# A two-block transformer kernel on one core: the first norm's row factors taken out of x and applied to the products

## The chip, the cores and the metric

The kernel runs on one core of a Trainium2 chip. The metric is device time in microseconds (us). One core has TensorE (PE, with its weight loads listed apart as PEld), VectorE (DVE), ScalarE (ACT), GpSimd (POOL), the queue engine SyncE (SP), and 16 DMA engines. SP issues nearly all DMAs. All arithmetic is float32 in meaning; large products are made from "leading" and "trailing" parts in the fp32r format.

## The reference, cut to what matters

Two blocks run one after the other on x, 256 tokens by 1024 features. The change touches the first norm and what is computed from it:

```
h    = x * rsqrt(mean(x*x, -1) + 1e-6) * norm_mix_g        # rmsnorm
proj = h @ w_in            # 1024 x 12296, split into
#  ml_q ml_k ml_v ml_o ml_i ml_f | sc_b sc_c sc_u | sb_q sb_k sb_v | g_ml g_sc g_sb
y_ml = head_rmsnorm(sigmoid(ml_o) * mlstm(ml_q, ml_k, ml_v, ml_i + b_i, ml_f + b_f))
y_sc = sc_b * causal_conv3(sc_c * sc_u)
y_sb = stick_breaking(sb_q, sb_k, sb_v)
merged = sigmoid(g_ml)*(y_ml @ w_ml) + sigmoid(g_sc)*(y_sc @ w_sc) + sigmoid(g_sb)*(y_sb @ w_sb)
x = x + merged @ w_out ; then an MLP, a norm, and a second block of like make-up
```

The factor rsqrt(...) is one number for each token (a "row factor"). As h enters the projections linearly, it can be applied to h or, later, to each product.

## The kernel before, in words

**Units and groups.** Every weight matrix is cut into groups of 512 output columns, and a group into units of up to 4 x 128 input rows. A unit is one 1 MB transfer (4 x 128 x 512 floats) into one of three landing buffers `land`. `UNITS` lists all of them in order, and all engines walk this one list. The first groups are sbq0, sbq1, sbk0, sbk1 and so on, two units each; groups alternate between two halves of the PSUM tensor `acc`.

**What happens to a unit.** SP issues its load (`load(u)`), waiting until the trailing part of unit u-3 is made. ACT copies `land` to `whi` in fp32r (the leading part, `hi_ready`), DVE subtracts it from `land` to get `wlo` (the trailing part, `lo_ready`); both do this in `split(u)`, up to two units ahead of PE. PE then runs `product(u)`. For a "feat" group (output features on partitions) a unit of 4 tiles and 4 column blocks is 48 matmuls of 256 columns: for each tile and block `whi` with `xT_hi`, `whi` with `xT_lo`, `wlo` with `xT_hi`. So all of `whi`, `wlo`, `xT_hi` and `xT_lo` are wanted at once.

**The front.** SP issues x in two halves of 128 tokens (512 KB each), then `con` (identity, triangle and a block of minus ones, 192 KB), then the small vectors (`rows`: 83 rows of 128 floats, 41.5 KB), then units 0 and 1, then five small tensors. ACT sums the squares of x; GpSimd makes `rstd` by `inverse_root`; ACT scales the first 128 tokens of x into `tok` and DVE the other 128. PE transposes the vectors (line 795), DVE copies the result to `vecs`, and PE transposes the scaled x (`turn`, line 591), 16 transposes in four pairs of tiles. `turn_split` turns each pair into `xT_hi` (ACT, times the gain vector) and `xT_lo` (DVE). Unit 0 is split in two halves, so that PE can begin at `half_lo`, the trailing half of the first weight.

```
        pe.wait_ge(norm_act, 1)
        pe.wait_ge(norm_dve, 1)
        pe.wait_ge(vecs_ready, 1)
        turn("x", tok)
```

After unit 0 PE makes a small table from `hot` and `rel33` (line 878); after unit `U_IF` = 1 it makes the two gate rows of the mLSTM (`if_gates`); DVE and ACT work on these at fixed distances from `U_IF`.

**Group ends.** When a group's last unit is done, DVE or ACT reads `acc` in one instruction of 128x1024: a copy or multiplication to sbqT, sbkT, mlqT, mlkT (line 1745), sbv and mlv, cT; an exponential for mlo; a sigmoid for the gates; then the gated products into `tok` (lines 1798 to 1801). The group after the next uses the same half of `acc`. After the last gated product PE transposes `merged` (`turn("merged", tok, half=1)`, inside unit out0) for which it waits on DVE.

**Later norms** already take their factors out of the transposed operand: `make_diag`, `spread` (line 600) and `take_row` turn a column of factors into `row`, the factor of every token on all partitions, which `along` repeats. They run twice, for stages 3 and 5.

The order of the work is written out by hand in the loops over `u`; nothing plans it.

Of the kernel before, what the change touches and what calls it, by code (L numbers as in the profile page):

```python
# [11 lines left out]
P = 128  # L12
# [160 lines left out]
U_IF = 1  # L173
# [9 lines left out]
def build(nc, dram, out):  # L183
# [24 lines left out]
    rstd = sb("rstd", [P, 7, TT], side="right")  # L208
    factor3 = sb("factor3", [P, TT], side="right")
# [141 lines left out]
    norm_act, norm_dve = sem("norm_act"), sem("norm_dve")  # L351
# [112 lines left out]
    def _(pe):  # L464
# [37 lines left out]
        def product(u, between):  # L502
# [12 lines left out]
            if u == 0:  # L515
                pe.wait_ge(half_lo, 1)
            if name == "gu2":
                pe.wait_ge(row_ready, 2)
            for k in range(m):
                if k == (m // 2 if u == 0 else 0):  # L520
# [21 lines left out]
                else:  # L542

                    for c in range(w // P):
# [7 lines left out]
                                  skip_group_check=True)  # L552
            last.then_inc(units_done, 1)
# [226 lines left out]
        def lru_gates():  # L780
            pe.wait_ge(l_conv, 1)
            pe.wait_ge(late_in, LATE)
            pe.wait_ge(row_ready, 1)
# [26 lines left out]
        def between(u, k):  # L810
# [17 lines left out]
            if (u, k) == (B2, 2):  # L828
                pe.wait_ge(xg_ready, 2)
                turn("h3", tok, half=1)  # L830
            if (u, k) == (B2 + 1, 3):
                spread(0, "h3")
# [3 lines left out]
            if (u, k) == (FIRST_U["gu0"] + 1, 2):  # L836
                spread(1, "h4")
# [23 lines left out]
        for u in range(NU):  # L861
# [4 lines left out]
            if u in TILES_APART:  # L866
# [3 lines left out]
                for v in TILES_APART[u]:  # L870
                    tile_product(v, 1).then_inc(units_done, 1)
            else:
                product(u, between)
            if u == 0:
# [33 lines left out]
    def _(act):  # L908
# [33 lines left out]
        def scale(j, src, count):  # L942
            act.wait_ge(rstd_ready, j + 1)
            activate(tok[:, 0, :], src[:, 0, :], ACT.Copy, scale=rstd[:, j, 0:1]).then_inc(norm_act, 1)

        def turn_split(stage, hi, k_to=0, bank=0, half=None):
            _, kk, gain = [s for s in TURNS if s[0] == stage][0]
            more = 2 if stage == "h4" else 0
            for b in range(kk // 2) if half is None else (2 * half, 2 * half + 1):
# [176 lines left out]

        for t in range(TT):
# [17 lines left out]
        for u in range(NU):  # L1145
# [36 lines left out]
            if u == 0:  # L1182
# [3 lines left out]
                             [P, 2 * KD, 8, ML_H]), ACT.Copy).then_inc(if_hi, 1)  # L1186
                act.wait_ge(tab_done, 1)
# [24 lines left out]
            if i == 0:  # L1212
                act.wait_ge(tab_out, 16)
                activate(sums_r[:, :], con[:, K_TRI:K_TRI + 2 * P], ACT.Copy).then_inc(sums_ready, 1)
# [3 lines left out]
            if u - 1 in (LAST_U["mlo0"], LAST_U["mlo1"]):  # L1218
                j = int(u - 1 > LAST_U["mlo0"])
                product_done(f"mlo{j}")  # L1220
                activate(mlo[:, :, j * NG:(j + 1) * NG], acc[:, G_AT[f"mlo{j}"] % 2], ACT.Exp,
                         scale=-1.0).then_inc(read_act, 1)
# [10 lines left out]
            if ends and name[:3] in ("gsb", "gml", "gsc"):  # L1233
# [3 lines left out]
                activate(gate[:], acc[:, n % 2], ACT.Sigmoid).then_inc(read_act, 1)  # L1237
# [66 lines left out]
    def _(dve):  # L1304
# [19 lines left out]
        def scale(j, src):  # L1324
            dve.wait_ge(rstd_ready, j + 1)
            v.tensor_scalar(tok[:, 1, :], src[:, 1, :], rstd[:, j, 1:2], None, ALU.mult).then_inc(norm_dve, 1)

# [763 lines left out]
```

## Time and profile before

| | |
|---|---|
| time, median of 3 runs | 935.81 us (935.42 to 935.91) |
| profiled execution | 935.66 us, span 934.0 us |
| PE busy | 913.2 us, 98% of the span |
| DVE busy | 589.5 us, 63% |
| ACT busy | 478.9 us, 51% |
| DMA | 163.95 MB, mean 176 GB/s |

The span runs from the first to the last recorded instruction; the rest of the time lies around it. PE's busy share is high throughout: in the page's 40 slices only the first (5), the last (7) and one near 735 us (8) are below nine tenths. A timeline row gives start, duration, engine, line, operation, output and inputs, shape and count, and in brackets how long the engine sat idle before and what released it.

### The profile page before, as it was taken

The numbers are of one execution on the slowest core, as the hardware profiler recorded it, in microseconds if no ns is written. First come the engines' busy times: TensorE is split into PE (matmuls) and PEld (weight loads), VectorE is DVE, ScalarE is ACT, GpSimd is POOL, SyncE is SP. The second block draws the span as 40 slices with busy tenths as digits, with TensorE's granted clock in tenths as the row PEclk, the third lists the DMA queues.
The fourth block names the chain that finished last, engine by engine and source line by source line (L and its number), as shares of the span: only waits on it lengthen the run. The fifth ranks groups of instructions, "written<-read, shape, count | busy, mean of one in ns | idle before, by whom it ended". The sixth has DMA issues, their size and how long they took to land.

```text
span 934.0 us, 13028 instructions
## 1 busy us (share of the span) xinstructions
PE 913.2 (98%) x5411; PEld 799.1 (86%) x5411; DVE 589.5 (63%) x619; ACT 478.9 (51%) x539; POOL 44.5 (5%) x88
## 2 busy tenths in 40 slices
PE   5999999999999999999999999999999899999997
PEld 4998998789998888888988888899888798888886
DVE  5555555467887545556677745648886667777643
ACT  6333877883445334334645534356754565555441
POOL 1000111110010000000000000010000100000000
PEclk9999999999999999999999999999999899999999
DMA  8566544544255656555555555537722565555551
GB/s 263 203 229 229 175 137 136 178 136 135 91 181 188 206 193 191 206 189 203 176 184 180 180 189 199 196 96 218 239 91 91 165 197 180 180 181 203 190 170 46
DMA packets 99371, 163.95 MB, mean 176 GB/s; under 512 B 4832, under 2 KB 37315, under 8 KB 99184
## 3 DMA queue, kind: packets, MB, share of 16 engines
q1 hardware_dynamic: 99312, 163.11, 53.1%
q8 instruction: 43, 0.70, 0.3%
q14 instruction: 16, 0.13, 0.0%
HBM read 162.03 MB, written 3.16 MB: 177 GB/s over the span
## 4 chain that ended last, share of the span: by engine, by line
PE 93%; DVE 3%; DMA 1%; ACT 1%; issue 1%; POOL 0%; SPq 0%; DVEq 0%; ACTq 0%; POOLq 0%
PE acc L539 14%; PE acc L541 14%; PE acc L540 14%; PE acc L547 9%; PE acc L551 8%; PE acc L549 8%; PE m L531 7%; PE acc L531 6%; PE m L533 4%; PE acc L533 3%; PE m L591 1%; DMA land<-in_w_in 1%; DVE wlo L1321 1%; PE m L631 1%; PE m L618 1%
## 5 line engine op out<-in xcount | busy, mean ns | idle before, releaser
L1321 DVE TENSOR_TENSOR wlo<-land,whi 128x2048 fp32r<-128x2048 f32 (+2 forms) x153 | 337.4, 2209 | 188.3 <-ACT whi L928 187.8
L928 ACT ACTIVATE whi<-land 128x2048 fp32r<-128x2048 f32 (+2 forms) x153 | 282.0, 1848 | 214.1 <-PE acc L541 152.7
L547 PE MATMUL acc<-xT,whi 128*128 128x256 f32 x656 | 189.9, 289 | 1.3 <-DVE xT L1604 0.8
L551 PE MATMUL acc<-xT,wlo 128*128 128x256 f32 x656 | 186.6, 284 | 0.0
L549 PE MATMUL acc<-xT,whi 128*128 128x256 f32 x656 | 186.6, 284 | 0.0
L547 PEld LDWEIGHTS acc<-xT,whi 128*128 128x128 f32 x656 | 126.7, 193 | 6.5 <-issue 4.4
L549 PEld LDWEIGHTS acc<-xT,whi 128*128 128x128 f32 x656 | 126.8, 193 | 0.2
L551 PEld LDWEIGHTS acc<-xT,wlo 128*128 128x128 f32 x656 | 126.8, 193 | 0.0
L531 PE MATMUL m<-xT,whi 128*128 128x512 f32 x288 | 102.2, 399 | 0.0
L539 PE MATMUL acc<-whi,xT 128*128 128x512 f32 (+2 forms) x240 | 91.5, 381 | 0.0
L540 PE MATMUL acc<-wlo,xT 128*128 128x512 f32 (+2 forms) x240 | 90.2, 376 | 0.0
L541 PE MATMUL acc<-whi,xT 128*128 128x512 f32 (+2 forms) x240 | 90.1, 376 | 0.0
L533 PE MATMUL m<-xT,wlo 128*128 128x256 f32 x288 | 80.9, 281 | 0.0
L531 PE MATMUL acc<-xT,whi 128*128 128x512 f32 x224 | 79.5, 399 | 0.0
L531 PEld LDWEIGHTS m<-xT,whi 128*128 128x128 f32 x288 | 54.1, 188 | 13.4
L533 PE MATMUL acc<-xT,wlo 128*128 128x256 f32 x224 | 62.9, 281 | 0.0
L533 PEld LDWEIGHTS m<-xT,wlo 128*128 128x128 f32 x288 | 54.4, 189 | 0.0
L539 PEld LDWEIGHTS acc<-whi,xT 128*128 128x128 f32 x240 | 45.1, 188 | 9.4 <-issue 1.0
L541 PEld LDWEIGHTS acc<-whi,xT 128*128 128x128 f32 x240 | 45.1, 188 | 8.3
L540 PEld LDWEIGHTS acc<-wlo,xT 128*128 128x128 f32 x240 | 45.1, 188 | 7.8
L531 PEld LDWEIGHTS acc<-xT,whi 128*128 128x128 f32 x224 | 42.1, 188 | 10.5
L539 PE MATMUL acc<-whi,aT_hi 128*128 128x512 f32 x128 | 49.9, 390 | 0.0
(385 smaller groups left out, 1350.8 us busy)
## 6 DMA issues: line engine op xcount, KB each, us to landing
land<-in_w_in SPq DMA_DIRECT2D x56, 1024.0 KB, 5.0
land<-in_w_up SPq DMA_DIRECT2D x16, 1024.0 KB, 5.2
land<-in_w_down SPq DMA_DIRECT2D x16, 1024.0 KB, 5.0
land<-in_w_ffn_gate SPq DMA_DIRECT2D x22, 512.0 KB, 3.7
land<-in_w_ffn_up SPq DMA_DIRECT2D x22, 512.0 KB, 4.7
land<-in_w_ffn_down SPq DMA_DIRECT2D x10, 1024.0 KB, 5.1
land<-in_w_out SPq DMA_DIRECT2D x6, 1024.0 KB, 5.0
land<-in_w_in SPq DMA_DIRECT2D x12, 512.0 KB, 3.7
```

The source lines that it names most:

```text
L531: mm(to, whi[:, s, k, cs], xT[:, k0 + k].rearrange("p a t -> p (a t)"), start=first, stop=False, skip_group_check=True)
L533: last = mm(to[:, 0:T], wlo[:, s, k, cs], xh[:, k0 + k, :], start=False, stop=end, skip_group_check=True)
L539: mm(to, xh[:, k0 + k, ts], whi[:, s, k, 0:w], start=first, stop=False)
L540: mm(to, xh[:, k0 + k, ts], wlo[:, s, k, 0:w], start=False, stop=False)
L541: last = mm(to, xl[:, k0 + k, ts], whi[:, s, k, 0:w], start=False, stop=end)
L547: mm(to, whi[:, s, k, cs], xh[:, k0 + k, :], start=first and c % 2 == 0, stop=False, skip_group_check=True)
L549: mm(to, whi[:, s, k, cs], xl[:, k0 + k, :], start=False, stop=False, skip_group_check=True)
L551: last = mm(to, wlo[:, s, k, cs], xh[:, k0 + k, :], start=False, stop=end, skip_group_check=True)
L591: last = nc.tensor.transpose(M[bank + b][:, (i * TT + t) * P:(i * TT + t + 1) * P], src[:, t, col0 + k * P:col0 + (k + 1) * P], ident)
L618: mm(M[(h + i) % 4][:, 0:T], sbkT[hs, c, 0:P], sbqT[hs, c, :], start=True, stop=True)
L928: activate(whi[:, u % PARTS, 0:m, 0:w], land[:, u % LANDS, 0:m, 0:w], ACT.Copy).then_inc(hi_ready, 1)
L1321: v.tensor_tensor(wlo[:, u % PARTS, 0:m, 0:w], land[:, u % LANDS, 0:m, 0:w], whi[:, u % PARTS, 0:m, 0:w].bitcast(F32), ALU.subtract).then_ ...
```

## The change

- PE transposes x as it came (`turn("x", x_tok)`); both `scale` functions and their semaphores go.
- `con`'s identity and the vectors are issued by ACT ahead of its first activation; `con`'s other two thirds by SP after unit 1.
- Unit 0 comes in two transfers of 512 KB with a semaphore each (`half_in`, `landed[0]`).
- Units 0 and 1 use `first_product`: first all products with the leading part `whi` (pair by pair, `xT_hi` then `xT_lo`), then those with `wlo`. The 48 matmuls of a unit stay 48.
- PE starts with 11 matmuls of 128x512 on a tile of ones, whose results nobody reads.
- The row factors come later: `make_diag(0, 0)`, `spread(0, "x")` after unit 1, `take_row(0)`, its square `row_sq` on DVE, and `minus_rstd` on GpSimd. Feature groups are multiplied by `row` (cT by `row_sq`, which also serves scu; scb's factor goes into psc), token groups are read in two instructions of 128x512 with `rstd` as the scalar.
- `U_IF` goes from 1 to 2, the table product from behind unit 0 to behind unit 1.

```diff
@@ SP
         for t in range(TT):
             sp.dma_start(x_tok[:, t, :], dram["x"][t * P:(t + 1) * P, :]).then_inc(x_in[t], 16)
-        sp.dma_start(con[:], dram["con"]).then_inc(con_in, 16)
-        sp.dma_start(rows[0:V_ROWS, :], dram["vectors"]).then_inc(rows_in, 16)
...
+            if u == 0:
+                (col, w), = segs
+                for half, sem_of in enumerate((half_in, landed[0])):
+                    ks = slice(half * UK // 2, (half + 1) * UK // 2)
+                    sp.dma_start(land[:, 0, ks, :], weights[weight][ks.start * P:ks.stop * P, col:col + w].rearrange(
+                        "(k p) n -> p k n", p=P)).then_inc(sem_of, 16)
+                return
...
             if u == 1:
+                sp.dma_start(con[:, P:], dram["con"][:, P:]).then_inc(ones_in, 16)
@@ PE
+        def first_product(u):
+            s, k0 = u % PARTS, UNITS[u][1]
+            def over(k, weight, moving, opens=False, ends=False):
+                for c in range(NG // P):
+                    to = acc[:, 0, c // 2, (c % 2) * T:(c % 2 + 1) * T]
+                    last = mm(to, weight[:, s, k, c * P:(c + 1) * P], moving[:, k0 + k, :],
+                              start=opens and c % 2 == 0, stop=ends, skip_group_check=True)
+                return last
+            for b in range(UK // 2):
+                if u == 0 and b == 0:
+                    pe.wait_ge(half_hi, 1)
+                else:
+                    pe.wait_ge(hi_ready, u + 1)
+                pe.wait_ge(turn_hi, k0 // 2 + b + 1)
+                for k in (2 * b, 2 * b + 1):
+                    over(k, whi, xT_hi, opens=k0 + k == 0)
+                pe.wait_ge(turn_lo, k0 // 2 + b + 1)
+                for k in (2 * b, 2 * b + 1):
+                    over(k, whi, xT_lo)
+            for k in range(UK):
+                if u == 0 and k == 0:
+                    pe.wait_ge(half_lo, 1)
+                elif k == (UK // 2 if u == 0 else 0):
+                    pe.wait_ge(lo_ready, u + 1)
+                last = over(k, wlo, xT_hi, ends=k0 + k == KD - 1)
+            last.then_inc(units_done, 1)
...
+        pe.wait_ge(heat_set, 1)
+        for _ in range(11):
+            mm(M[3][:, :], ymlT_hi[:, 0, 0:P], ymlT_hi[:, 0:2, :].rearrange("p a b -> p (a b)"), start=True, stop=True)
         pe.wait_ge(con_in, 16)
         pe.wait_ge(rows_in, 16)
         nc.tensor.transpose(M[0][:, 0:V_ROWS], rows[0:V_ROWS, :], ident[0:V_ROWS, 0:V_ROWS]).then_inc(vecs_turned, 1)
-        pe.wait_ge(norm_act, 1)
-        pe.wait_ge(norm_dve, 1)
+        for t in range(TT):
+            pe.wait_ge(x_in[t], 16)
         pe.wait_ge(vecs_ready, 1)
-        turn("x", tok)
+        turn("x", x_tok)
...
+            if (u, k) == (1, UK):
+                pe.wait_ge(ones_in, 16)
+                spread(0, "x")
@@ ACT
+        act.dma_start(con[:, 0:P], dram["con"][:, 0:P]).then_inc(con_in, 16)
+        act.dma_start(rows[0:V_ROWS, :], dram["vectors"]).then_inc(rows_in, 16)
...
-        act.wait_ge(sq_act, 1)
-        scale(0, x_tok, 1)
         act.wait_ge(vecs_ready, 1)
+        turn_split("x", xT_hi, only=(0,))
+        act.wait_ge(half_in, 16)
+        activate(whi[:, 0, 0:UK // 2, :], land[:, 0, 0:UK // 2, :], ACT.Copy).then_inc(half_hi, 1)
+        turn_split("x", xT_hi, only=(1,))
         act.wait_ge(landed[0], land_count(0))
-        activate(whi[:, 0, 0:UK // 2, :], land[:, 0, 0:UK // 2, :], ACT.Copy).then_inc(half_hi, 1)
-        turn_split("x", xT_hi, half=0)
         activate(whi[:, 0, UK // 2:, :], land[:, 0, UK // 2:, :], ACT.Copy).then_inc(hi_ready, 1)
         turn_split("x", xT_hi, half=1)
         split(1)
...
-                activate(gate[:], acc[:, n % 2], ACT.Sigmoid).then_inc(read_act, 1)
+                for t in range(TT):
+                    last = activate(gate[:, t], acc[:, n % 2, t], ACT.Sigmoid, scale=rstd[:, 0, t:t + 1])
+                last.then_inc(read_act, 1)
@@ DVE
-        scale(0, x_tok)
+        dve.wait_ge(vecs_ready, 1)
+        turn_split("x", xT_hi, xT_lo, only=(0,))
         dve.wait_ge(half_hi, 1)
-        dve.wait_ge(landed[0], land_count(0))
+        dve.wait_ge(half_in, 16)
         v.tensor_tensor(wlo[:, 0, 0:UK // 2, :], land[:, 0, 0:UK // 2, :], whi[:, 0, 0:UK // 2, :].bitcast(F32),
                         ALU.subtract).then_inc(half_lo, 1)
-        dve.wait_ge(vecs_ready, 1)
-        turn_split("x", xT_hi, xT_lo, half=0)
+        turn_split("x", xT_hi, xT_lo, only=(1,))
...
         split(1)
+        make_diag(0, 0)
...
+            if u == 1:
+                take_row(0)
+                dve.wait_ge(row_ready, 1)
+                v.tensor_tensor(row_sq[:, :], row[:, :], row[:, :], ALU.mult)
...
-                v.tensor_scalar(to[:, 4 * j:4 * j + 4, :].rearrange("p a b -> p (a b)"), flat, by, None,
-                                ALU.mult).then_inc(read_dve, 1)
+                v.scalar_tensor_tensor(out=to[:, 4 * j:4 * j + 4, :], in0=flat.rearrange("p (a b) -> p a b", b=T),
+                                       scalar=by, in1=along(4), op0=ALU.mult, op1=ALU.mult).then_inc(read_dve, 1)
...
+                    if name[:3] == "psc":
+                        for t in range(TT):
+                            last = v.scalar_tensor_tensor(out=gated[:, t], in0=acc[:, n % 2, t],
+                                                          scalar=rstd[:, 0, t:t + 1], in1=gate[:, t], op0=ALU.mult,
+                                                          op1=ALU.mult)
+                        link(last)
@@ GpSimd
+        signal(g.memset(ymlT_hi[:, 0:2, :].bitcast(F32), 1.0), heat_set)
         link(g.memset(mhalf[:], -0.5))
         signal(g.memset(rel33[BUCKETS:BUCKETS + 1, :], 1.0), pool_set)
         inverse_root(0, [(sq_act, 1)])
+        signal(g.tensor_scalar(minus_rstd[:, :], rstd[:, 0, :], -1.0, None, ALU.mult), minus_ready)
```

## Rows read from the trace of the kernel before

**Rows 1.** The page, part 1: PE's busy time, share and instructions.

```profile
PE 913.2 (98%) x5411; PEld 799.1 (86%) x5411; DVE 589.5 (63%) x619; ACT 478.9 (51%) x539; POOL 44.5 (5%) x88
```

**Rows 2.** Waits: engine, line, what it waited for: us, times, longest.

```profile
PE m L795 <- DMA diag<-in_vectors: 8.8, 1, 8.8
```

**Rows 3.** Timeline of SP, first 12 us.

```profile
0.79 0.86 SPq L398 DMA_DIRECT2D x_tok<-in_x  x2
2.17 0.33 SPq L400 DMA_DIRECT2D diag<-in_vectors  x1
2.54 2.35 SPq L410 DMA_DIRECT2D land<-in_w_in  x2
```

**Rows 4.** Timeline of PE, first 21 us.

```profile
8.81 0.37 PE L795 MATMUL m<-con,diag 83*128 83x83 f32 x1 [8.81 <-DMA diag<-in_vectors]
10.30 3.65 PE L591 MATMUL m<-con,tok 128*128 128x128 f32 x16 [1.12 <-DVE tok L1326]
14.42 0.36 PE L547 MATMUL acc<-xT,whi 128*128 128x256 f32 x1 [0.47 <-DVE xT L1359]
...
20.33 1.02 PE L878 MATMUL m<-hot,rel 33*8 33x512 f32 x2
```

**Rows 5.** Timeline of ACT, first 20 us.

```profile
4.66 1.06 ACT L1129 ACTIVATE tok<-x_tok 128x1024 f32<-128x1024 f32 x1 [2.60 <-DMA x_tok<-in_x]
...
6.00 1.06 ACT L1129 ACTIVATE tok<-x_tok 128x1024 f32<-128x1024 f32 x1 [0.18 <-DMA x_tok<-in_x]
...
11.17 1.06 ACT L1139 ACTIVATE whi<-land 128x1024 fp32r<-128x1024 f32 x1 [1.58 <-DMA land<-in_w_in]
12.14 1.55 ACT L957 ACTIVATE xT<-m,vecs 128x256 fp32r<-128x256 f32 x4
...
15.93 3.77 ACT L928 ACTIVATE whi<-land 128x2048 fp32r<-128x2048 f32 x2
```

**Rows 6.** DMA view, packets by size: 6.5 to 8.0 us, then 8.0 to 8.5.

```profile
DMA packets 299, 0.53 MB, mean 353 GB/s; under 512 B 0, under 2 KB 54, under 8 KB 299
DMA packets 89, 0.18 MB, mean 356 GB/s; under 512 B 2, under 2 KB 2, under 8 KB 89
```

**Rows 7.** Timeline of DVE, 9 to 23 us.

```profile
9.30 0.24 DVE L1639 COPY vecs<-m 128x83 f32<-128x83 f32 x1 [3.02 <-PE m L795]
9.46 0.74 DVE L1326 TENSOR_SCALAR tok<-x_tok,rstd 128x1024 f32<-128x1024 f32 x1
...
13.41 1.65 DVE L1359 SCALAR_TENSOR_TENSOR xT<-m,vecs,xT 128x256 fp32r<-128x256 f32 x4
...
17.92 4.49 DVE L1321 TENSOR_TENSOR wlo<-land,whi 128x2048 fp32r<-128x2048 f32 x2 [0.16 <-ACT whi L928]
```

**Rows 8.** Transposes of line 591 (ns min/median/max): of x at 10.3, of mlo at 277 us.

```profile
L591 PE MATMUL m<-con,tok x16: 421/421/447, 10.3 to 13.5; 128*128 128x128 f32 x16
L591 PE MATMUL m<-con,mlo x16: 272/272/273, 277.6 to 279.2; 128*128 128x128 f32 x16
```

**Rows 9.** Timeline of GpSimd at 8 us.

```profile
8.41 0.52 POOL L1968 MEMSET sel_r<- 36x512 f32 x1
```

**Rows 10.** Windows on PE: stretch, length, busy (count), granted clock, DMA share, GB/s.

```profile
734.40:739.56 5.16, 1.97 (x10) 0.85 0.57 197
739.56:744.60 5.04, 5.04 (x23) 0.50 0.00 0
```

**Rows 11.** Timeline of PE around the first spread.

```profile
630.75 0.61 PE L600 MATMUL m<-diag,con 128*128 128x128 f32 x4
631.12 0.36 PE L547 MATMUL acc<-xT,whi 128*128 128x256 f32 x1
```

**Rows 12.** Groups on DVE by form: count, busy us, mean ns, idle before.

```profile
L1620 DVE SCALAR_TENSOR_TENSOR mixed<-acc,rstd,gain_b 128x512 f32<-128x512 f32 x4 | 2.9, 748 | 9.5 <-ACT tok L985 9.5
```

**Rows 13.** Timeline of DVE and PE behind the last gated product.

```profile
418.03 1.22 DVE L1801 TENSOR_TENSOR tok<-tok,gated 128x1024 f32<-128x1024 f32 x1
...
419.31 1.09 PE L591 MATMUL m<-con,tok 128*128 128x128 f32 x8
```

More of the change, by code:

```diff
@@ L172 @@
 GATE0 = SB0 + SB_H
-U_IF = 1
+U_IF = 2
 TURN_SB = ML0 + 6
@@ L208, in build @@
     rstd = sb("rstd", [P, 7, TT], side="right")
+    minus_rstd = sb("minus_rstd", [P, TT], side="right")
+    row_sq = sb("row_sq", [P, T], side="right")
     factor3 = sb("factor3", [P, TT], side="right")
@@ L830, in between @@
                 turn("h3", tok, half=1)
+            if (u, k) == (1, UK):
+                pe.wait_ge(ones_in, 16)
+                spread(0, "x")
             if (u, k) == (B2 + 1, 3):
-                spread(0, "h3")
+                spread(1, "h3")
             if (u, k) == (FIRST_U["gu0"], 2):
@@ L836, in between @@
             if (u, k) == (FIRST_U["gu0"] + 1, 2):
-                spread(1, "h4")
+                spread(2, "h4")
             if (u, k) == (B2 + 4, 4):
@@ L940, in square, with turn_split @@
             act.wait_ge(sq_act, squares_done[0])
[L942 to L946, printed above, removed]
+        def turn_split(stage, hi, k_to=0, bank=0, half=None, only=None):
             _, kk, gain = [s for s in TURNS if s[0] == stage][0]
             more = 2 if stage == "h4" else 0
-            for b in range(kk // 2) if half is None else (2 * half, 2 * half + 1):
+            for b in only or (range(kk // 2) if half is None else (2 * half, 2 * half + 1)):
                 act.wait_ge(turned, TURN_AT[stage] + b + 1 + more)
@@ L1220, in _ @@
                 product_done(f"mlo{j}")
-                activate(mlo[:, :, j * NG:(j + 1) * NG], acc[:, G_AT[f"mlo{j}"] % 2], ACT.Exp,
-                         scale=-1.0).then_inc(read_act, 1)
+                act.wait_ge(minus_ready, 1)
+                for t in range(TT):
+                    last = activate(mlo[:, t, j * NG:(j + 1) * NG], acc[:, G_AT[f"mlo{j}"] % 2, t], ACT.Exp,
+                                    scale=minus_rstd[:, t:t + 1])
+                last.then_inc(read_act, 1)
             if i % 2 == 1 and 3 <= i <= SB_H + 1:
@@ L1345, in along, with turn_split @@
             return row[:, :].unsqueeze(1).to_broadcast([P, k, T])
-        def turn_split(stage, hi, lo, k_to=0, bank=0, half=None):
+        def turn_split(stage, hi, lo, k_to=0, bank=0, half=None, only=None):
             _, kk, gain = [s for s in TURNS if s[0] == stage][0]
             more = 2 if stage == "h4" else 0
-            for b in range(kk // 2) if half is None else (2 * half, 2 * half + 1):
+            for b in only or (range(kk // 2) if half is None else (2 * half, 2 * half + 1)):
                 dve.wait_ge(turn_hi, TURN_AT[stage] + b + 1 + more)
@@ L1666, in _ @@
                 turn_split("h3", xT_hi, xT_lo, half=1)
-                make_diag(0, 3)
+                make_diag(1, 3)
             if u == FIRST_U["gu0"]:
@@ L1672, in _ @@
                 turn_split("h4", xT_hi, xT_lo, half=1)
-                make_diag(1, 5)
+                make_diag(2, 5)
             if u - SB0 in range(4, SB_H + 3, 2):
@@ L1749, in _ @@
                 product_done(name)
-                if name[0] == "s":
-                    last = v.tensor_copy(sbv[:, :, j * NG:(j + 1) * NG], acc[:, n % 2])
-                else:
+                if name[0] == "m":
                     v.memset(mlv[:, :, 2 * j:2 * j + 2, ML_D:ML_D + 1], 1.0)
-                    last = v.tensor_copy(mlv[:, :, 2 * j:2 * j + 2, 0:ML_D],
-                                         acc[:, n % 2].rearrange("p t (h d) -> p t h d", d=ML_D))
+                for t in range(TT):
+                    if name[0] == "s":
+                        to, src = sbv[:, t, j * NG:(j + 1) * NG], acc[:, n % 2, t]
+                    else:
+                        to = mlv[:, t, 2 * j:2 * j + 2, 0:ML_D]
+                        src = acc[:, n % 2, t].rearrange("p (h d) -> p h d", d=ML_D)
+                    last = v.tensor_scalar(to, src, rstd[:, 0, t:t + 1], None, ALU.mult)
                 last.then_inc(read_dve, 1)
@@ L1799, in _ @@
                 else:
-                    link(v.tensor_tensor(gated[:], acc[:, n % 2], gate[:], ALU.mult))
+                    if name[:3] == "psc":
+                        for t in range(TT):
+                            last = v.scalar_tensor_tensor(out=gated[:, t], in0=acc[:, n % 2, t],
+                                                          scalar=rstd[:, 0, t:t + 1], in1=gate[:, t], op0=ALU.mult,
+                                                          op1=ALU.mult)
+                        link(last)
+                    else:
+                        link(v.tensor_tensor(gated[:], acc[:, n % 2], gate[:], ALU.mult))
                     v.tensor_tensor(m, m, gated[:], ALU.add).then_inc(read_dve, 1)
```

36 lines of the change are left out of this document (19 added, 17 removed).

## Prediction

> **What bounds the kernel now.** The page first: PE is busy 98% of the span [rows 1], so only PE's stalls and added or removed PE work can move the time. The waits view comes next: its longest entry on PE is 8.8 us before the first transpose, for the DMA of the vectors [rows 2]. The rest is in the timeline of the first 20 us, engine by engine. The SP timeline [rows 3] gives the issue order x, x, (con,) vectors, first weight. The vectors' transpose starts at 8.81, the 16 transposes of x at 10.30, the first product at 14.42, and from there PE runs without a gap until the table product at 20.33 [rows 4]. So the front of 14.42 us is the prize; everything in the change outside it can only cost.
>
> Why do the vectors land at 8.78 although they were issued at 2.17, when the second half of x, issued under a microsecond earlier, is used at 6.00 [rows 3, 5]? The DMA view: from 6.5 to 8.0 us 54 packets of 512 B pass, and none of that size from 8.0 to 8.5 [rows 6]. That is 28 ns each, 18 GB/s: about what one of 16 engines moves when all move 353 GB/s (22 each), not what 16 would. So I take it that the 83 rows of the vectors run on one engine, 83 x 28 ns = 2.3 us, done at 8.0, landing 0.8 later. It also explains why ACT gets the 1 MB weight only at 11.17, 8.6 us after its issue [rows 3, 5]: on that engine it starts at 8.0 and takes 64 KB at some 25 GB/s, 2.6 us. The Trainium skill (DMA: Bandwidth & Descriptors, section "Why a DMA increments its semaphore by 16 and not by 1") says the number of engines is the largest up to 16 that divides the outer dimension, so that 83, a prime, gets one; by that rule too moving the issue to another queue spreads nothing.
>
> **The change part by part.** Start of the chain. Norm: the row factors leave the front: DVE's scaling of 9.46 to 10.20 was what the transposes waited for [rows 7], and ACT's, as long, goes too. The transposes now need x, con and the vectors. The con part before them is a third (64 of 192 KB; 128 KB at 0.4 MB per us is 0.3 us). Issuing from ACT saves no engine work: the one engine still has to move its part of x, con and all 83 rows before the transposes can start. So the later of x and vectors lands at 8.78 - 0.3 = 8.5. Low bound: the 83 rows cost nothing, which leaves x and con, 6.2; high bound under the rivals.
>
> From there: before, landing to the end of the vecs copy was 9.54 - 8.78 = 0.76 [rows 7], plus 0.08 to wake PE: transposes start at 9.35 (before 10.30, after DVE's scaling). Four transposes take 0.6 us at the full clock (16 records in 1.91 at 277 us is 0.107 apart plus the tail; 272 ns each [rows 8]), 1.1 at half (421 ns [rows 8]). ACT then splits the first pair, half of 1.55, 0.78, and copies half a weight, 1.06 [rows 5]; with 0.15 for semaphores the leading half is ready at 9.35 + 0.6 + 0.78 + 1.06 + 0.15 = 11.95. (Where x is the later of the two, ACT has its second square, 1.06 + 0.19, before the pair, but the pair doesn't wait for the transposes: 8.5 + 1.25 + 0.78 + 1.06 + 0.15 = 11.75, the same.) The half weight itself lands one 0.5 MB after x on the slow engine: x halves are 6.00 - 4.66 = 1.34 apart [rows 5], so 8.5 + 1.34 = 9.85, in time for 10.75. The first product no longer waits for DVE's trailing parts (before, whi to product took 14.42 - 12.23 = 2.2). New start 12.0: gain 14.42 - 12.0 = 2.4.
>
> Unread matmuls. GpSimd's memset of 128x512 (36x512 took 0.52 [rows 9]; 0.4 to 0.8 either way) lets PE start at 1.4. At half clock 24 matmuls of 256 columns took 5.04 us [rows 10], so 11 of 512 columns take 11 x 0.42 = 4.6: end 6.1, before the vectors, so they delay nothing. Their use is the clock: the x transposes ran 421 ns each, at 1.2 GHz, where the later ones ran 272, at 2.4 [rows 8] (the granted-clock column shows 1.00 there, so the durations decide). After 734.4 us the clock is at 0.85 on average over 5.16 us, so it fell about 1.5 us before the end, near 738.0, 3.6 us after the last dense matmul; it stayed at 0.50 for the 5.04 us of dense work behind [rows 10]. In the front it had risen 4.2 us after the transposes began. So 4.6 us of unread matmuls are about enough to raise it, and the pause of 6.1 to 9.35 is 3.25, just under 3.6. I take the clock as kept, with chance 6 in 10.
>
> Does the rest keep up behind the earlier start S? ACT: 0.78 + 1.06 + 1.55 + 1.9 [rows 5] puts the second weight's leading part at S + 5.4 with waits, PE wants it at S + 5.8 (48 matmuls, 14.42 to 20.33 less the issue [rows 4]). Cover 0.4; if it is gone, up to 0.4 lost. DVE: 1.2 + 0.83 + 1.2 + 1.65 + 2.25 is S + 7.7 with waits (the halves of the weight taken as half of 2.25), wanted at S + 9.6 [rows 7]. The product's own count of matmuls and order cost nothing: same pairs, same 0.12 pace. The transfers behind: SP issues one more weight half and con's rest (0.4 us each) ahead of the small ones and unit 2. The small ones are wanted two units later than they land, unit 2 after S + 13. The table product moves behind unit 1, same price.
>
> Added on PE: the row spread, four records at 630.75, the next product's first matmul at 631.12, 0.36 long instead of 0.28: 0.37 + 0.08, 0.45 us [rows 11]. It waits for make_diag, done by DVE 5 us earlier. Added on DVE and ACT: groups of 128x1024 are read as two of 128x512, 0.75 each on DVE [rows 12] against 1.23, some 0.27 more, and about that on ACT; the banks are read a whole group (11 us) before PE wants them, so this is hidden. At one place there is no cover: the second gated product of the last branch. DVE's addition starts at 418.03 (and ends 419.25), PE's transposes start at 419.31 [rows 13]. Two instructions instead of one push it by 0.1 to 0.27; I take 0.1. Where a product with the row takes the place of a copy, both read 1024 elements in one instruction: nothing.
>
> Sum: -2.4 + 0.45 + 0.1 = -1.85, say 1.9 less. The profiled execution took 935.66 (span 934.0 and 1.66 around); the median is 935.81, 0.15 above. 935.8 - 1.9 = 933.9. Own range: landing 8.2 to 8.8, ACT's cover 0.4, the last branch 0 to 0.2: 933.3 to 934.8.
>
> **Rivals.** (1) The clock is lost in the pause. The 16 transposes take 3.65 again: from 9.35 to 13.0, start at 13.05, the first matmuls still slow (0.2). Gain 14.42 - 13.25 = 1.2, less 0.55, leaves 0.65: 935.2. For it: the pause is nearly as long as the one at 734 us, where some transposes even lay inside. Against: the rows' 3.6.
>
> (2) Slower: the vectors starve. Two queues now share the slow engine. If it takes one packet from each in turn, each 512 B row waits for a packet of x (4 KB) or weight (2 KB) of SP's queue, which is full: 8 + 8 of x, 16 + 16 of the halves, 32 of unit 1. Eight con packets go first, so 72 of 83 rows have passed at the end of unit 1. That is x's end on the engine, 5.2 (6.00 less the 0.8 from last packet to landing), plus 2 MB more at 1.34 per 0.5 MB, 5.4, plus 2.3 of its own: 12.9, landed 13.7. Transposes 14.55 with the clock long fallen, 3.65: start 18.25, 3.8 later, with 0.55 and 0.3 of slow matmuls: 940.4. It decides from a landing of 9.3 (half clock) or 10.4 (full) on. For it: the queue is really full in that stretch, and only one row per packet goes. Against: no row here shows two queues at once, and an engine that shared by bytes or by whole transfers would land them near 8.5 to 9.8. The Trainium skill (same page, section "Queues, rings and completion order") says an engine round-robins between queues, packet by packet, with some 9 to 17 descriptors in one: by single rows it would be this rival, by such packets it would be a landing near the forecast's.
>
> (3) The vectors don't bind: if my reading of the one engine is wrong and they land with con at about 6.2, transposes start at 7.0, ACT is free at 7.15 after the second square, its pair done 8.4, weight copied 9.5, start 9.6: gain 4.8 - 0.55, 931.6. Against: 54 packets in 1.5 us.
>
> **Chances.** Forecast 0.40, clock lost 0.20, starved 0.22, not binding 0.12, something between or a new stall 0.06. The range must hold the starved case: 931.6 to 940.4. A measurement here tells about 0.2%, 1.87 us, from no change: below 933.94 is faster. Half of the forecast's case and all of (3) lie there: 0.36; same, the other half, (1) and part of the rest: 0.38; slower: 0.26.
>
> **What would show it.** The start of the vectors' transpose: 8.5 right, 6 rival 3, over 10 rival 2. The duration of the x transposes: 272 or 421 ns. The first product: 12.0. ACT's half copy directly behind its first pair, and no idle on PE between the first and third unit. The spread 0.45. If the first product starts at 12.0 and the time is not 1.9 lower, my reading that nothing behind the front stalls is wrong.

## The result

The changed kernel takes **937.36 us** (median of 20 runs, 936.71 to 939.64), the kernel before 935.96 us (20 runs beside them, 935.02 to 938.27): ratio 1.0015, 95% interval 1.0008 to 1.0022. It is slower by 1.4 us. The forecast was 933.9.

The profiled execution took 937.64 us, span 935.9 (before 934.0). The page, part 1, has PE busy 5.4 us longer [rows 1], nearly all of it the unread matmuls:

```profile
PE 918.6 (98%) x5426; PEld 803.2 (86%) x5426; DVE 591.2 (63%) x628; ACT 479.8 (51%) x546; POOL 46.9 (5%) x90
```

The wait for the vectors looks shorter than 8.8 us [rows 2] in the view of the waits:

```profile
PE m L834 <- DMA diag<-in_vectors: 4.9, 1, 4.9
```

This is a trap: the wait starts later, behind the unread matmuls. The timeline of PE shows the time at which it ends:

```profile
1.36 4.91 PE L831 MATMUL m<-ymlT_hi 128*128 128x512 f32 x11 [1.36 <-POOL ymlT_hi L2027]
11.19 0.37 PE L834 MATMUL m<-con,diag 83*128 83x83 f32 x1 [4.92 <-DMA diag<-in_vectors]
12.06 3.65 PE L627 MATMUL m<-con,x_tok 128*128 128x128 f32 x16 [0.50 <-DVE vecs L1684]
...
15.36 4.45 PE L568 MATMUL acc<-xT,whi 128*128 128x256 f32 x32
...
27.41 1.02 PE L922 MATMUL m<-hot,rel 33*8 33x512 f32 x2
28.36 0.71 PE L636 MATMUL m<-diag,con 128*128 128x128 f32 x4
28.83 0.37 PE L553 MATMUL acc<-xT,whi 128*128 128x256 f32 x1
```

Against [rows 4], the vectors' transpose starts at 11.19 instead of 8.81, and the first product at 15.36 instead of 14.42. The norm did leave the chain (x's transposes follow the vectors after 0.9 us, before after 1.5), and the product starts 0.3 us behind the first leading half, where it was 2.2 before, but the late landing eats both.

The vectors were issued 0.9 us earlier than before [rows 3] and landed 2.4 us later. The timeline of ACT, which now issues them, shows x's second half late as well, 7.26 against 6.00 [rows 5]:

```profile
1.24 0.54 ACTq L1168 DMA_DIRECT2D diag<-in_vectors  x1
...
7.26 1.06 ACT L1171 ACTIVATE tok<-x_tok 128x1024 f32<-128x1024 f32 x1 [1.40 <-DMA x_tok<-in_x]
...
13.97 1.06 ACT L1180 ACTIVATE whi<-land 128x1024 fp32r<-128x1024 f32 x1
```

The DMA view by queue shows why. q1 is SP's queue, q10 is ACT's (con's 128 rows and the vectors' 83). The columns are packets, MB and share of 16 engines. First 4 to 5 us, in which the last of con's packets still pass:

```profile
q1 hardware_dynamic: 103, 0.39, 95.2%
q10 hardware_dynamic: 70, 0.03, 10.7%
```

Then 5 to 6, and 7 to 8 us:

```profile
q1 hardware_dynamic: 172, 0.37, 99.2%
q10 hardware_dynamic: 4, 0.00, 0.8%
...
q1 hardware_dynamic: 192, 0.38, 104.0%
q10 hardware_dynamic: 9, 0.00, 1.6%
```

From 5.0 us on, 4 to 9 packets of ACT's queue pass in a microsecond, until 10.5 us. 192 packets on 16 engines are 12 for each engine and microsecond, 83 ns each. If a row takes the 28 ns of the kernel before [rows 6], nine rows leave an engine time for nine such packets: one for one on a single engine, about 110 ns a row. Before 5.0 us it was different. From 4.4 to 5.0 us, behind con's rows, the vectors' rows passed at 26 ns each, though SP's queue was as full:

```profile
q1 hardware_dynamic: 59, 0.24, 99.9%
q10 hardware_dynamic: 23, 0.01, 6.5%
```

The granted clock on PE by stretches (length, busy, count, clock, DMA share, GB/s) shows the second loss:

```profile
6.30:11.20 4.90, 0.01 (x1) 0.81 1.05 370
11.20:15.40 4.20, 3.70 (x18) 0.50 0.88 244
```

The granted clock reads 1.00 up to 9.2 us and 0.50 from 9.4 on: it fell 3.1 us into the pause of 4.9 behind the unread matmuls. They had only just raised it. Of the eleven (shortest, median and longest in ns), the last alone took less than 628, so the 1.00 at the start of the column is not to be trusted:

```profile
L831 PE MATMUL m<-ymlT_hi x11: 477/628/792, 1.4 to 5.8; 128*128 128x512 f32 x11
```

At the lower level the transposes of x take the same 421 ns as before [rows 8] (1.2 GHz), and the first 32 products 4.45 us in place of 4.06 to 4.09, the time they take in the runs below that kept the clock.

How it adds up, with the help of e12 below, a run that kept the clock and whose first product starts at 14.42 as before. The first group product behind the front, on DVE, comes at 41.66 before, at 42.14 in e12 (the spread: +0.48) and at 43.43 here. The 1.29 between the last two are the later first product, +0.94, and its slow start, +0.35 (units 0 and 1 take 12.05 us in place of 11.70). Together: +1.77. Before, then after:

```profile
41.66 1.23 DVE L1745 TENSOR_SCALAR sbqT<-acc 128x1024 f32<-128x1024 f32 x1 [1.46 <-PE acc L551]
```

```profile
43.43 1.23 DVE L1796 SCALAR_TENSOR_TENSOR sbqT<-acc,row 128x1024 f32<-128x1024 f32 x1 [2.87 <-PE acc L557]
...
420.04 1.23 DVE L1863 TENSOR_TENSOR tok<-tok,gated 128x1024 f32<-128x1024 f32 x1
```

The addition at 420.04 is 2.01 later than before [rows 13], and the gated product ahead of it 1.82 later (418.59 after 416.77), so the last gated product in two instructions cost about 0.2. The spans differ by 1.9, the medians by 1.4; single executions of one kernel differ by that much.

### The profile page after: what moved, and what is told of

It reads as the page before. It is cut to its first block, busy times and chain, and to the rows that moved or that the text cites. A ratio compares the mean times of both kernels' runs of the same rounds, so it can differ in the third digit from the quotient of the medians.

```text
span 935.9 us, 13083 instructions
## 1 busy us (share of the span) xinstructions
PE 918.6 (98%) x5426; PEld 803.2 (86%) x5426; DVE 591.2 (63%) x628; ACT 479.8 (51%) x546; POOL 46.9 (5%) x90
## 4 chain that ended last, share of the span: by engine, by line
PE 93%; DVE 3%; DMA 1%; ACT 1%; issue 1%; POOL 0%; ACTq 0%; DVEq 0%; POOLq 0%
PE acc L545 14%; PE acc L546 14%; PE acc L547 14%; PE acc L553 8%; PE acc L555 8%; PE acc L557 8%; PE m L537 7%; PE acc L537 6%; PE m L539 4%; PE acc L539 3%; PE m L627 1%; PE acc L568 1%; DMA diag<-in_vectors 1%; DVE wlo L1370 1%; PE m L667 1%
## 5 line engine op out<-in xcount | busy, mean ns | idle before, releaser
L553 PE MATMUL acc<-xT,whi 128*128 128x256 f32 x624 | 180.8, 290 | 0.9 <-DVE xT L1649 0.9
L555 PE MATMUL acc<-xT,whi 128*128 128x256 f32 x624 | 177.5, 285 | 0.0
L557 PE MATMUL acc<-xT,wlo 128*128 128x256 f32 x624 | 177.4, 284 | 0.0
L553 PEld LDWEIGHTS acc<-xT,whi 128*128 128x128 f32 x624 | 120.6, 193 | 4.9 <-issue 3.7
L555 PEld LDWEIGHTS acc<-xT,whi 128*128 128x128 f32 x624 | 120.7, 193 | 0.2
L557 PEld LDWEIGHTS acc<-xT,wlo 128*128 128x128 f32 x624 | 120.6, 193 | 0.0
L539 PE MATMUL acc<-xT,wlo 128*128 128x256 f32 x224 | 62.9, 281 | 0.0
L537 PEld LDWEIGHTS acc<-xT,whi 128*128 128x128 f32 x224 | 42.1, 188 | 10.5
```

Source lines behind the costliest of these rows:

```text
L537: mm(to, whi[:, s, k, cs], xT[:, k0 + k].rearrange("p a t -> p (a t)"), start=first, stop=False, skip_group_check=True)
L539: last = mm(to[:, 0:T], wlo[:, s, k, cs], xh[:, k0 + k, :], start=False, stop=end, skip_group_check=True)
L553: mm(to, whi[:, s, k, cs], xh[:, k0 + k, :], start=first and c % 2 == 0, stop=False, skip_group_check=True)
L555: mm(to, whi[:, s, k, cs], xl[:, k0 + k, :], start=False, stop=False, skip_group_check=True)
L557: last = mm(to, wlo[:, s, k, cs], xh[:, k0 + k, :], start=False, stop=end, skip_group_check=True)
```

## Experiments

The theory after the two traces: the vectors' rows, on one engine, pass one by one between the packets of SP's full queue (cause of the late landing), and the pause that this leaves loses the clock. The rivals: ACT's issue or the size of the rows is slow by itself; the clock doesn't matter, since the product hangs on ACT. All kernels are built on the changed one unless said. Ratios are against the kernel before, run beside them. e1, e2, e3, e7 and e8 are on the landing, e4, e5, e10 and e12 on the clock, e6, e9 and e11 on who waits for what.

**e1_sp_queue: the vectors issued by SP.**

```diff
@@ SP, behind x
+        sp.dma_start(con[:, 0:P], dram["con"][:, 0:P]).then_inc(con_in, 16)
+        sp.dma_start(rows[0:V_ROWS, :], dram["vectors"]).then_inc(rows_in, 16)
@@ ACT
-        act.dma_start(con[:, 0:P], dram["con"][:, 0:P]).then_inc(con_in, 16)
-        act.dma_start(rows[0:V_ROWS, :], dram["vectors"]).then_inc(rows_in, 16)
```

> The changed kernel with the identity part of con and the vectors issued by SP between x and the first weight, as before, instead of by ACT. Theory (the single engine that carries the 83 rows shares itself between two queues, so the rows wait behind the weight): in one queue they come right behind x, the vectors' transpose starts at 8.5 instead of 11.19, x lands at 6.0 instead of 7.26, the first product starts at 12.0 to 13.1 (was 15.36), and the time falls by 2.3 to 3.4 us to 934.0 to 935.1. Rival (which queue issues them is indifferent, the one engine alone decides): no change from 937.4.

Measured: 934.75 us, ratio 0.9993 (0.9984 to 1.0001). Timeline of PE:

```profile
8.47 0.26 PE L836 MATMUL m<-con,diag 83*128 83x83 f32 x1 [2.25 <-DMA diag<-in_vectors]
9.24 3.60 PE L629 MATMUL m<-con,x_tok 128*128 128x128 f32 x16 [0.51 <-DVE vecs L1684]
12.51 4.16 PE L570 MATMUL acc<-xT,whi 128*128 128x256 f32 x32
```

The landing of 8.5 that the forecast counted on is that of SP's queue. Moving the issue back is worth 2.6 us. The transposes start at 9.24 (forecast 9.35), but behind a pause of 2.25 us the clock fell here too, just as they began (granted 0.68 from 9.2 to 9.4 us, 0.50 from there), and the product started at 12.51, not 12.0. Against the kernel before the interval just includes no change.

**e2_80_rows: the vectors as 80 + 3 rows, still from ACT.**

```diff
-        act.dma_start(rows[0:V_ROWS, :], dram["vectors"]).then_inc(rows_in, 16)
+        for r0, r1 in ((0, 80), (80, V_ROWS)):
+            act.dma_start(rows[r0:r1, :], dram["vectors"][r0:r1, :]).then_inc(rows_in, 16)
```

> The changed kernel with the vectors moved in two transfers, 80 rows and 3 rows, both from ACT. Theory (83 rows go to one engine because of their count): 80 rows spread over 16 engines, 5 each, so they land with con near 5 us, x lands at 6.0 to 6.3, the unread matmuls end at 6.3, the transposes of x start at 7.05 at 272 ns each, the half weight lands at 7.6, the first product starts at 9.6 and the time is 931.6. Rival (small packets of the second queue wait whatever the engine): the vectors land after 9 us and the time stays over 936. Rival (the weight, not the vectors, is late then): half weight after 9, time 933.

Measured: 931.59 us, ratio 0.9957 (0.9944 to 0.9969): 5.8 us under the changed kernel from one more DMA. Timeline of PE:

```profile
6.33 0.26 PE L834 MATMUL m<-con,diag 83*128 83x83 f32 x1 [0.27 <-DMA diag<-in_vectors]
7.09 1.94 PE L627 MATMUL m<-con,x_tok 128*128 128x128 f32 x16 [0.50 <-DVE vecs L1685]
9.65 4.09 PE L568 MATMUL acc<-xT,whi 128*128 128x256 f32 x32 [0.62 <-ACT whi L1181]
```

**e3_before_80: the kernel before, its vectors as 80 + 3 rows from SP.**

> The kernel before with one edit alone: its vectors in two transfers, 80 rows and 3 rows, from SP. Theory: they land at 6.6 instead of 8.78, DVE's scaling of x then follows the row factors at 8.4, the transposes start at 9.6 instead of 10.3, the first weight lands at 9.3 instead of 11.1, the first product starts at 13.3 instead of 14.42: 1.0 us less than before, 934.9. Rival (the one engine is not what made the weight late): the weight still lands at 11.1 and the time stays at 936.0 or falls by no more than 0.3.

Measured: 934.04 us, ratio 0.9987 (0.9978 to 0.9995). Timelines of PE, then ACT:

```profile
6.68 0.37 PE L796 MATMUL m<-con,diag 83*128 83x83 f32 x1 [6.68 <-DMA diag<-in_vectors]
9.43 3.68 PE L592 MATMUL m<-con,tok 128*128 128x128 f32 x16 [2.38 <-ACT tok L945]
```

```profile
9.34 1.06 ACT L1140 ACTIVATE whi<-land 128x1024 fp32r<-128x1024 f32 x1
```

The vectors land 2.1 us earlier, and ACT no longer waits for the weight (11.17 before [rows 5], 9.34 here). So 83 rows on one engine held up both, in the kernel before too. The gain is only 1.7 us because the norm then binds (2.38 us for ACT's scaling). The two cures help each other: the rows alone give 1.7 us here, the norm's removal with late vectors 1.0 at most (e1, not clear of nothing), both together 4.1 (e2).

**e4_no_unread: without the 11 unread matmuls and their memset.**

> The changed kernel without the 11 unread matmuls and the memset of their operand. Theory: as the vectors land at 11.19, PE pauses 4.9 us behind the unread matmuls and the clock falls again (421 ns transposes), so they buy nothing and cost nothing: 937.4 within 0.3. Rival (their heat still helps the first product, whose clock rises sooner): 0.5 to 1.0 slower without them. Rival (they delay something): faster without them.

Measured: 937.79 us, ratio 1.0029 (1.0019 to 1.004); single runs lie between 935.78 and 939.64. The profiled one, the fastest, had the landing at 9.55 and 21 packets of ACT's queue between 5 and 6 us, where the changed kernel had 4. Whether that comes of the edit or of chance is not shown: each kernel has one trace, and the changed kernel, e10, e11 and e12, all with unread matmuls, landed at 11.09 to 11.23. For the changed kernel, whose clock is lost either way, the unread matmuls buy 0.7 us by the medians (each against the kernel before, run beside it), and the intervals overlap, so that nothing is clear.

**e5_80_no_unread: e2 without them.**

> The changed kernel with the vectors as 80 + 3 rows, without the 11 unread matmuls and their memset. Theory: with the vectors early, TensorE has no pause after the unread matmuls, and it is they that give the transposes of x their 272 ns in place of 421; without them the 16 transposes take 3.6 instead of 1.94 us (+1.7), and the first product starts up to 1.7 us later and at the lower clock level: 932.6 to 933.6 us against 931.6 with them. Rival: the first product waits for ScalarE's split and the weight, not for the transposes, so that at most 0.4 us is lost: 931.6 to 932.0.

Measured: 932.94 us, ratio 0.997 (0.9959 to 0.998), 1.35 more than e2. Timeline of PE:

```profile
7.14 3.65 PE L627 MATMUL m<-con,x_tok 128*128 128x128 f32 x16 [0.51 <-DVE vecs L1682]
10.44 5.25 PE L568 MATMUL acc<-xT,whi 128*128 128x256 f32 x32
```

The vectors' transpose is at 6.27 as in e2 (6.33), but the transposes of x take 421 ns, the product starts 0.8 later and its first 32 matmuls take 1.2 longer. Where no long pause follows, the unread matmuls are worth 1.9 us by the front of the trace and 1.35 by the medians.

**e7_weight_waits: SP issues the first weight only when the vectors have landed** (`sp.wait_ge(rows_in, 16)` ahead of unit 0's loads).

> The changed kernel (83 rows in one transfer from ScalarE's queue), but SyncE issues the first weight only when the vectors have landed. Theory (between 5 and 10.5 us the vectors' rows pass one by one between the packets of SyncE's queue): with no weight in that queue the last 44 rows take 28 ns each, as they do in the kernel before: the vectors land at 6.5 to 7.5 and not at 11.2, their transpose starts there, x's transposes at about 8; the first half of the weight, issued some 5 us later, lands at about 10 to 11, so that the first product starts at 12 to 13 in place of 15.4, and the time is 934.5 to 936. Rival (the one engine is held by something else than the weight's packets, such as x's, or the rows are slow by themselves): the vectors land after 9, everything is later than in the changed kernel, 941 us or more.

Measured: 935.37 us, ratio 0.9993 (0.9984 to 1.0002). DMA by queue, 5.6 to 6.4 and 6.5 to 7.3 us, then PE:

```profile
q1 hardware_dynamic: 4, 0.02, 6.2%
q10 hardware_dynamic: 4, 0.00, 0.8%
...
q10 hardware_dynamic: 34, 0.02, 7.2%
q1 hardware_dynamic: 1, 0.00, 0.1%
```

```profile
7.95 0.37 PE L835 MATMUL m<-con,diag 83*128 83x83 f32 x1 [2.40 <-DMA diag<-in_vectors]
...
12.81 4.90 PE L569 MATMUL acc<-xT,whi 128*128 128x256 f32 x32 [0.34 <-ACT whi L1181]
```

Only what stands behind x in SP's queue was taken away. Up to 6.4 us the last packets of x, 4 KB each, still pass one for one with the rows, 200 ns for each pair. Once they are through, the rows take 24 ns each in place of 110. The vectors were used at 7.95 (expected 6.5 to 7.5). The landing's cause is shown: the packets of the other queue beside them, and not a slow issue or small rows by themselves. Holding the weight back even beats the changed kernel by 2 us.

**e8_64_19_rows: e2 with 64 + 19 rows.**

> The changed kernel with the vectors as 64 + 19 rows. Theory (the number of rows divides over engines or goes to one of them): 64 rows go over 16 engines, four each, and 19 have one engine. By the pace of one row a SyncE packet (110 ns) 19 rows take 2.1 us where 3 rows took next to nothing, and the vectors land at 6.3 to 8.4 in place of 6.33: 931.6 to 933.7 us, nearer the first, since 39 rows had passed by 5 us in the changed kernel. Rival (what the 80 + 3 split won came from splitting in two, or from the smaller descriptors, not from the spread over the engines): the same as 83 rows in one, landing at 9 to 11, 937 us.

Measured: 934.71 us, ratio 0.9989 (0.998 to 0.9998); above the expected range. DMA by queue, 6 to 7 us (from 7 to 8 it was 7 packets of ACT's queue, then none), then PE:

```profile
q1 hardware_dynamic: 186, 0.36, 101.0%
q10 hardware_dynamic: 10, 0.01, 1.9%
```

```profile
8.46 0.37 PE L834 MATMUL m<-con,diag 83*128 83x83 f32 x1 [2.03 <-DMA diag<-in_vectors]
9.33 3.65 PE L627 MATMUL m<-con,x_tok 128*128 128x128 f32 x16 [0.50 <-DVE vecs L1685]
```

The 64 rows pass quickly (83 packets between 5 and 6 us), the 19 crawl at the pace of the changed kernel's last 44. None of the vectors' rows had passed by 5 us, so the 19 missed the easy time that I had counted on. The 2.1 us of lateness cost 3.1 us of time, for the clock was low as well: the transposes take 421 ns. Here it wasn't lost in the pause. All eleven unread matmuls took 628 ns or more, so in this execution they had not raised it at all, and the granted clock shows no fall:

```profile
L831 PE MATMUL m<-ymlT_hi x11: 628/628/795, 1.4 to 5.8; 128*128 128x512 f32 x11
```

Two transfers by themselves are not the whole cure (2.7 us won against the changed kernel, 5.8 with 80 + 3); the count of rows on the one engine decides the rest.

**e6_vector_half: e2, VectorE copies the first leading half** (a `tensor_copy` behind the copy of `vecs`, ACT's copy removed).

> The changed kernel with the vectors as 80 + 3 rows, and VectorE in place of ScalarE makes the leading parts of the first weight's first half. With 80 + 3 rows the first product began at 9.65, 0.62 us after its engine could have, waiting for ScalarE's copy (8.54 to 9.60) behind its split of the first turns. Theory: VectorE, free at 7.0, has the copy done by about 8.9, before the turns of x are all made, and the first product starts at 9.0: 931.0 us. Rival: VectorE's copy holds the trailing parts of x's turns and of the weight back by as much, so the second step of the product waits, and nothing is won: 931.6; or the half lands later than 8 and it is slower, 932.

Measured: 930.59 us, ratio 0.9947 (0.9935 to 0.996). The first product starts at 8.80 without a wait, VectorE's copy took 0.69 us against ACT's 1.06. The interval overlaps that of e2, so the step rests on the trace:

```profile
7.65 0.69 DVE L1685 CAST whi<-land 128x1024 fp32r<-128x1024 f32 x1 [0.70 <-DMA land<-in_w_in]
```

**e9_turn_while_copied: e6, the vectors transposed into `acc[:, 1, 0]`,** with PE's wait for `vecs_ready` behind `turn("x", x_tok)`.

> The version with 80 + 3 rows and VectorE's leading half (930.59 us), with the vectors' transpose in a bank of the accumulator that nothing uses yet, so that the transposes of x follow it at once and no longer wait 0.5 us for VectorE's copy of it. Theory: in that version the transposes (7.09 to 8.8) were the last thing before the first product at 8.80; they now start at about 6.5 and end at 8.2, and the first product waits for the half of the weight (landed 7.65, copied at 8.34): 8.4, a gain of 0.3 to 0.4 us: 930.2. Rival: ScalarE's split of the first turns stays behind its second sum of squares (to 7.5), and the first half is split at 7.8 in any case: nothing won, 930.6.

Measured: 930.04 us, ratio 0.9931 (0.9918 to 0.9944), the fastest version. Its interval overlaps that of e6, so only the trace tells the step: the first product 0.2 earlier. Timeline of PE:

```profile
6.57 1.94 PE L627 MATMUL m<-con,x_tok 128*128 128x128 f32 x16
8.60 4.07 PE L568 MATMUL acc<-xT,whi 128*128 128x256 f32 x32
```

**e10_20_unread: 20 unread matmuls instead of 11.**

> The changed kernel with 20 unread matmuls at the front in place of 11. The eleven take 4.91 us and end at 6.3; nine more at 0.43 us end at about 10.2, so that 1.0 us of pause is left before the vectors land, in place of 4.9. Theory: the clock fell in that pause and costs 1.0 to 1.6 us (the transposes of x at 421 in place of 272 ns, and the first 2 us of the product at the lower level; leaving the unread matmuls out with early vectors cost 1.3): 935.8 to 936.3 us against 937.4. Rival: the pause doesn't matter, since the product's start hangs on ScalarE's copies and what follows is paced by the splits: 937.0 to 937.4.

Measured: 937.34 us, ratio 1.0012 (1.0002 to 1.0023). Inconclusive: they ended at 8.40, a pause of 2.8 us remained, and the clock fell at about 12.9, in the middle of the transposes, so that the products ran slow (4.84 us for the first 32). The second nine took 0.24 us each, not the 0.43 that the expectation took.

**e12_30_unread: 30 of them.**

> The changed kernel with 30 unread matmuls at the front. With 20 of them they ended at 8.4 (the second nine took 0.24 us each, not 0.43), 2.8 us of pause were left, and the clock fell at 12.9, so that the run told little of the clock. At that pace 30 end at 10.8, just before the vectors land at 11.2. Theory (the clock costs the changed kernel 1.0 to 1.6 us): the transposes of x take 272 ns and end at 13.9, the first product starts at 14.5 as with 20, but runs at the full clock and is over at about 26.2 against 27.4, and the time is 935.9 to 936.3 us. Rival: what follows unit 1 is paced by the splits, whose times hang on the weight's landing, so that at most 0.4 us is won: 937.0 to 937.4. A landing earlier than 10.8, as it was without the unread matmuls, would be lost behind them: some runs then don't gain.

Measured: 935.7 us, ratio 0.9997 (0.9988 to 1.0006), 1.7 under the changed kernel, with the vectors as late as there. Timeline of PE:

```profile
11.09 0.26 PE L834 MATMUL m<-con,diag 83*128 83x83 f32 x1 [0.74 <-DMA diag<-in_vectors]
11.85 1.94 PE L627 MATMUL m<-con,x_tok 128*128 128x128 f32 x16 [0.51 <-DVE vecs L1684]
14.42 4.09 PE L568 MATMUL acc<-xT,whi 128*128 128x256 f32 x32 [0.63 <-ACT whi L1180]
```

The table product behind unit 1 comes at 26.12 against 27.41: the lost clock cost the changed kernel 1.3 us by the trace, 1.7 by the medians. (This profiled execution, 937.57, lies above its median. Its lead of 1.3 us over the changed kernel held to 696 us and fell to 0.5 by 703, where its granted clock was 0.76 and the changed kernel's 1.00; by 735 us it was gone. What lowered the clock there is not shown.)

**e11_x_before_vectors: x transposed first, the vectors into another bank when they land.**

> The changed kernel (83 rows in one transfer from ScalarE's queue), with x transposed before the vectors, which are transposed into another bank when they land. Theory: x's second half lands at 7.26, the transposes run from there to about 9.3 at 272 ns and are off the path; of the late vectors (11.2) only their transpose, VectorE's copy and ScalarE's splits are left behind them, and the first product starts at 13.3 to 14.0 in place of 15.4: 935.4 to 936.2 us. Rival: ScalarE's order (split, copy of the half, split) holds the product to the same time, or the clock falls all the same and the product takes that back: 937 us.

Measured: 937.21 us, ratio 1.0004 (0.9993 to 1.0014). The rival was right. Timeline of PE, then the clock by stretches:

```profile
7.38 1.94 PE L627 MATMUL m<-con,x_tok 128*128 128x128 f32 x16 [1.27 <-DMA x_tok<-in_x]
11.15 0.29 PE L837 MATMUL acc<-con,diag 83*128 83x83 f32 x1 [1.83 <-DMA diag<-in_vectors]
13.71 6.51 PE L568 MATMUL acc<-xT,whi 128*128 128x256 f32 x32 [2.27 <-ACT whi L1180]
```

```profile
11.10:13.70 2.60, 0.29 (x1) 0.76 0.76 131
13.70:17.00 3.30, 3.29 (x15) 0.50 0.71 269
```

The product started 1.65 us earlier, as expected, and was over 0.4 later (27.82 against 27.41): the transposes no longer stood between the pause and the product, so the whole time at 1.2 GHz fell on the products.

## Why the prediction was wrong

**The step that failed** is "So the later of x and vectors lands at 8.78 - 0.3 = 8.5". It treated the one engine's work as a sum that any queue gets through in the same time. It was 11.19 in the changed kernel; e1, with the same bytes and the same engine but SP's queue, has 8.47, and e7, with ACT's queue but no weight beside it, 7.95. What decides is what stands in the other queue, and how large its packets are.

That is rival 2, the starved vectors, with the price too high: 13.7 and 940.4. From 5.0 us on its rule held, one row for one packet. But by then 39 of the 83 rows were through (183 of the 228 packets, taking con's 128 and its 16 semaphore writes as passed), the last 23 of them at 26 ns each, a pace that leaves the engine no time for x's packets between them. The 39 at 28 ns are 1.1 us of the engine, about what x's second half lost (1.26). The last 44 took 5.4 us: 4 in the first, 40 at 110 ns. That gives 10.4 for the last and, with 0.8, 11.2 for the landing. Why the first 39 went in one run is open. It is not loose chance: by the same count 39 or 40 rows had passed when the pace changed in e7, e10, e11 and e12, but 61 in e4. Nor is it the size of the packets beside them: in e7 the run ends at 4.8 us, while x's 4 KB packets go on to 6.4.

The prediction had named a landing of 9.3 to 10.4 as the point of no gain; e1 at 8.47 and e4's profiled run at 9.55 (935.78) fit it. The Trainium skill (DMA: Bandwidth & Descriptors, section "Queues, rings and completion order") speaks of packets of some 9 to 17 descriptors in the turns between queues. The trace disagrees from 5.0 us on, in the changed kernel and in e8: near one row for each packet of the other queue. Turns of some size may lie in the run of the first 39, which no row here can divide. Had such turns held to the end, the landing would have been near the forecast's.

**The second step, smaller:** "I take the clock as kept, with chance 6 in 10". It was lost: 3.1 us into the pause here, at the start of x's transposes in e1, 2.3 us behind the last unread matmul in e7 (granted 0.53 from 7.8 to 8.0 us). Nor were the unread matmuls as surely enough as the forecast had it: they raised the clock only with the last of them here, and not at all in e8. They took 4.91 us, not 4.6 ([rows 10] has 23 matmuls in 5.04 us; the sum took 24). So even with the landing of 8.5 the time would have been e1's 934.75, not 933.9. Rival 1's 935.2 for that case was near, its product start (13.05) 0.5 too late. Reading the pause at 734 us as a limit of 3.6 was wrong: some matmuls ran in it, and in the front shorter idle stretches were enough.

**What held.** The vectors' 83 rows do run on one engine (e2, e3, e8). The case in which they don't bind was put at 931.6 with a product at 9.6; e2 measured 931.59 and 9.65. With the clock and the vectors in time, ACT's order was right: pair, half weight, product. PE had no idle time between the first and third units (96 matmuls back to back), so the later start was passed on unchanged. The unread matmuls delayed nothing (end 6.27). Spread: 0.48 by e12, where 0.45 was taken. Last gated product: 0.2 where 0.1 was taken. The chance of an unchanged time within 0.2% (0.38) covers the result; the sign of the forecast was wrong.

## What to carry to other kernels

A small transfer whose rows can't be divided over the engines sits on one of them: cut off the remainder (80 + 3) before anything else is moved, and keep what is left as short as can be, for it pays per row. A second queue was no shortcut beside a full one: for over half of its rows the small transfer paid one large packet each. Where a late start and a raised clock depend on each other, price both together: a start won by shortening the chain was given back when the pause grew (e11), and unread matmuls paid only where they reached to the work (e5, e12) and were enough to raise the clock at all (not in e8).

## What was not expected of the hardware

- Two queues on one engine: 9 rows of 512 B per us beside full 2 KB packets (about 110 ns each), one row in 200 ns beside 4 KB packets, 24 ns each once the other queue is empty (e7), 28 ns in SP's own queue [rows 6].
- Before it came to one for one, a run of rows passed at 26 ns each beside a queue as full. It ended after 39 or 40 rows, at 4.8 to 5.0 us, in five kernels, and after 61, at 5.6 us, in e4, whose landing was 9.55. The times of e4's executions spread from 935.8 to 939.6.
- Unread matmuls of 128x512 took 0.45 us each at first (11 in 4.91) and 0.21 from the twelfth on (30 in 8.98). Eleven of them raised the clock near their end (4.19 us in all in e7, 4.91 here) or not at all (5.06 in e8).
- The granted clock fell after idle stretches of 2.25 us (e1), 2.3 (e7) and 3.1 us (the changed kernel), and once, after a pause of 2.8 us, during the dense work that followed it (e10). It stayed up over 0.74 us between 30 unread matmuls and the vectors (e12) and over 1.27 us between 11 of them and the transposes (e11).
